# Forget gates of a hybrid attention layer: an addition and a running sum on VectorE become one scan with two additions

## The reference, cut to what matters

```python
log_f = jax.nn.log_sigmoid((f_logit + b_forget[layer]).astype(jnp.float32))
log_f_cum = jnp.cumsum(log_f.transpose(0, 2, 1), axis=-1)
...
logits = logits + log_f_cum[:, :, start:end, None] - log_f_cum[:, :, None, :end]
```

## Time and profile before

| | before |
|---|---|
| median of 3 runs | 803.08 us |
| the profiled execution | 803.57 us |
| its span, first to last instruction | 801.8 us |
| PE busy | 792.6 us (99%) |
| DVE busy | 580.4 us (72%) |
| ACT busy | 454.9 us (57%) |
| POOL busy | 239.2 us (30%) |
| share of PE in the chain that ended last | 94% |

### The profile page before, as it was taken

How to read it: one execution, slowest core, us unless ns; L and a number is a source line. 1 busy time by engine, 2 the same in 40 slices (tenths; PEclk the granted TensorE clock), 3 DMA queues, 4 the chain that set the end, 5 groups by cost and what they waited for, 6 DMA issues and landing times.

```text
span 801.8 us, 12113 instructions
## 1 busy us (share of the span) xinstructions
PE 792.6 (99%) x4184; PEld 671.3 (84%) x4184; DVE 580.4 (72%) x1178; ACT 454.9 (57%) x928; POOL 239.2 (30%) x378
## 2 busy tenths in 40 slices
PE   9999999999999999999999999999999999999997
PEld 8878888888888888888888888888888888888885
DVE  6877666676668887767788776779657677875575
ACT  7767665556647555665745576565546483542232
POOL 0112631342245225234533341454233111410000
PEclk9999999999999999999999999999999999999999
DMA  9414823114122411411061131104312298152532
GB/s 345 155 53 151 273 80 117 54 41 131 40 79 51 134 40 67 132 39 54 30 175 46 67 103 69 53 27 114 110 54 67 82 371 300 54 179 79 184 132 105
DMA packets 35276, 88.93 MB, mean 111 GB/s; under 512 B 3592, under 2 KB 11784, under 8 KB 34192
## 3 DMA queue, kind: packets, MB, share of 16 engines
q1 hardware_dynamic: 35216, 88.17, 33.3%
HBM read 57.72 MB, written 21.53 MB: 99 GB/s over the span
## 4 chain that ended last, share of the span: by engine, by line
PE 94%; DVE 2%; DMA 2%; issue 1%; ACT 1%; SPq 0%; ACTq 0%; DVEq 0%
PE banks L818 16%; PE banks L820 16%; PE banks L819 16%; PE banks L863 11%; PE banks L993 9%; PE banks L1013 5%; PE banks L980 5%; PE banks L1012 5%; PE banks L979 5%; PE banks L1064 1%; PE banks L950 1%; PE banks L945 1%; PE banks L1033 1%; DMA hT<-wo_dram 1%; PE banks L935 1%
## 5 line engine op out<-in xcount | busy, mean ns | idle before, releaser
L818 PE MATMUL banks<-hT,w_parts 128*128 128x512 f32 x576 | 237.3, 412 | 0.2 <-DVE sb_heads L1661 0.2
L820 PE MATMUL banks<-hT,w_parts 128*128 128x512 f32 x576 | 225.9, 392 | 0.0
L819 PE MATMUL banks<-hT,w_parts 128*128 128x512 f32 x576 | 225.4, 391 | 0.0
L1775 DVE TENSOR_TENSOR pT<-banks,pT 128x512 fp32r<-128x512 f32 x208 | 108.3, 563 | 88.9 <-ACT pT L1222 87.3
L1222 ACT ACTIVATE pT<-banks 128x512 fp32r<-128x512 f32 x208 | 92.5, 497 | 135.3 <-PE banks L993 135.1
L820 PEld LDWEIGHTS banks<-hT,w_parts 128*128 128x128 f32 x576 | 108.1, 188 | 24.5
L818 PEld LDWEIGHTS banks<-hT,w_parts 128*128 128x128 f32 x576 | 108.5, 188 | 15.0 <-DVE sb_heads L1661 0.7
L819 PEld LDWEIGHTS banks<-hT,w_parts 128*128 128x128 f32 x576 | 108.9, 189 | 13.3
L1490 POOL TENSOR_TENSOR w_parts<-w_raw,w_parts 128x1024 fp32r<-128x1024 f32 x34 | 81.5, 2398 | 95.9 <-ACT w_parts L1122 95.9
L1735 DVE TENSOR_TENSOR_SCAN work<-work 128x639 f32<-128x639 f32 (+3 forms) x64 | 90.6, 1416 | 4.7 <-POOL work L1497 4.6
L1198 ACT ACTIVATE work<-banks 128x512 f32<-128x512 f32 (+2 forms) x96 | 47.5, 495 | 71.0 <-PE banks L980 60.8
(11 more groups left out here) (248 smaller groups left out, 1366.3 us busy)
## 6 DMA issues: line engine op xcount, KB each, us to landing
w_raw<-in_w_tiles SPq DMA_DIRECT2D x36, 512.0 KB, 4.1
hT<-wo_dram SPq DMA_DIRECT2D x14, 512.0 KB, 8.0
fx_heads<-fx_heads SPq DMA_DIRECT2D x8, 512.0 KB, 7.5
negL<-negL_dram SPq DMA_DIRECT2D x8, 512.0 KB, 6.5
yT_dram<-silu SPq DMA_DIRECT2D x8, 512.0 KB, 5.1
sb_heads<-sb_heads SPq DMA_DIRECT2D x8, 512.0 KB, 7.0
negL<-yT_dram SPq DMA_DIRECT2D x8, 512.0 KB, 5.0
work<-in_x SPq DMA_DIRECT2D x6, 512.0 KB, 7.0
```

What stands on the lines that cost most here:

```text
L818: pe.matmul(o, w[0][:, k, :], hT[:, 0, k, tok], start=(k == 0), stop=False)
L819: pe.matmul(o, w[0][:, k, :], hT[:, 1, k, tok], start=False, stop=False)
L820: mm = pe.matmul(o, w[1][:, k, :], hT[:, 0, k, tok], start=False, stop=(k == KT - 1))
L1775: dve.tensor_tensor(pT[:, n % 3, 1, cols], banks[:, T_BANK + n % 2, cols], pT[:, n % 3, 0, cols].bitcast(F32), ALU.subtract).then_inc(t_lo, 1)
```

## The change

`f_one` and its filling (L1947) go. `forget_sum` goes, and `forget_scan` runs in tick 2 in place of tick 3, right behind ACT's logarithm: state = (f_a + state) + f_m. SP's store stands at its tick 3 in place of 4; its order of DMAs is the same as before.

```diff
-FORGET_SUM, FORGET_SCAN, FORGET_STORE = 2, 3, 4
+FORGET_SCAN, FORGET_STORE = 2, 3
...
-            def forget_sum():
+            def forget_scan():
+
                 dve.wait_ge(f_ln, 1)
-                dve.tensor_tensor(f_m, f_m, f_a, ALU.add).then_inc(f_sum, 1)
-
-            def forget_scan():
-                dve.wait_ge(f_sum, 1)
-                dve.tensor_tensor_scan(f_m, f_one, f_m, 0.0, ALU.mult, ALU.add).then_inc(f_scan, 1)
+                dve.tensor_tensor_scan(f_m, f_a, f_m, 0.0, ALU.add, ALU.add).then_inc(f_scan, 1)
...
-            link(dve.memset(f_one, 1.0))
             forget_begin(0)
...
-                if i == FORGET_SUM:
-                    forget_sum()
                 if i == FORGET_SCAN:
                     forget_scan()
```

More of the change, by code:

```diff
@@ L450, in hybrid_layer @@
         junk, junk_dve = pT[:, 0, :, :], pT[:, 1, :, :]
-        f_u, f_one, f_a, f_m = work[0:FH, S:2 * S], work[0:FH, 2 * S:3 * S], f_row(0)[0:FH, :], f_row(1)[0:FH, :]
+        f_u, f_a, f_m = work[0:FH, S:2 * S], f_row(0)[0:FH, :], f_row(1)[0:FH, :]
         wo_rows = [(silu[:, :], negL[:, 0, :])] + [(raw, fx_heads[:, i * S:(i + 1) * S].bitcast(F32)) for raw, i in
@@ L512, in hybrid_layer @@
         wf_hi, wf_lo = sem("wf_hi"), sem("wf_lo")
-        f_abs, f_exp, f_ln, f_sum, f_scan, negL_out = sem("f_abs"), sem("f_exp"), sem("f_ln"), sem("f_sum"), sem("f_scan"), sem("negL_out")
+        f_abs, f_exp, f_ln, f_scan, negL_out = sem("f_abs"), sem("f_exp"), sem("f_ln"), sem("f_scan"), sem("negL_out")
         negL_in = [sem("negL_in0"), sem("negL_in1")]
```

## The result

The changed kernel takes 804.59 us (median of 22 runs, 803.6 to 805.36), the kernel before 803.34 us (median of 22, 802.88 to 804.12): a ratio of 1.0013, with a 95% interval of 1.0007 to 1.0019. (The medians differ by 1.25 us, a quotient of 1.0016; the ratio is not taken from them alone, and its interval holds both.) It is slower by 0.6 to 1.5 us, which is less than the 0.2% that the text ahead calls no change; still, with 22 runs of each, a ratio of 1 lies outside the interval. The profiled execution took 804.53 us with a span of 802.8, where the one before had 803.57 and 801.8.

A forecast was written before the change was run, and what follows sets the result against it. PE, busy 792.6 of 801.8 us, was taken as the bound, with DVE counting only where PE waits. Terms -0.35 + 1.3 + 0 = +0.95 us on the 803.08 median gave 804.03, predicted 804.0, range 802.5 to 804.8.

The forecast's parts named there:

- The two waits of PE: PE's waits for DVE at L818 (0.35 us late) and L1012 (0.48 us late), together at most 0.83 us to gain.
- The maximum of unit 3: DVE's result that ACT's exponential awaits; predicted 1.00 us later, since what stands between units 2 and 3's maxima sets time.
- The scan takes 2.27 us, held it ends 2.14 behind POOL: DVE's new scan at about 65.3 us, 2.27 us by itself, held by POOL's subtraction L1490, ending at 69.04.
- The stall at unit 5: New PE wait of some 1.3 us at the scores of unit 5, for ACT's exponential of unit 3.
- The terms of the sum: On PE: -0.35 at L818, +1.3 at the scores of unit 5 (the 0.35 included), 0 at L1012: +0.95 us.
- The filling gives its 0.35 back: Removing DVE's 0.91 us filling ahead of L1661 gains 0.35 us at L818, given back at the scores of unit 5.
- the logarithm's chain: Steps behind the last forget logits, up to 65 us; predicted at most 0.14 us earlier without the filling, 0.05 taken.
- The scan that is not held: Rival: POOL does not hold the scan, it ends at 67.61, maximum of unit 3 0.43 us earlier; 802.65 us, chance 0.12.
- the slow scan: Rival: two additions make the scan slower, up to 3.34 us, for +2.02 or 805.10 us; chance 0.08.
- Both waits of PE gone: Rival: keys do not hang on ACT's queue, so all 0.83 us at L818 and L1012 is gained; 802.25 us, chance 0.04.
- SP's store is worth nothing: SP's store goes at about 69.1 in place of 70.77; read only from tick 32, so no gain.
- The fetch that moves along with PE: PE's only wait after 74 us, 0.7 us, for a fetch SP issues when PE reaches a point of its program.

## Why the prediction was right

It forecast 804.0 us in 802.5 to 804.8, a loss of 0.95 us; measured were 804.59 and a loss of 1.25 (0.6 to 1.5).

- **The two waits of PE are all that can be gained.** The mechanism is shown: with the scan in tick 3 both are gone. But the 0.83 us that the text calls the most that PE can gain was too small: PE gained 0.94 us at L1012 and 1.09 behind it. It left out that the matmuls behind a wait also come late, by 0.1 us and more (55.37 behind 55.03 is 0.34 us, and 54.80 behind 54.58 is 0.22 with the wait gone).
- **The maximum of unit 3 sets the time.** Shown from three sides: more work between the scan and it costs in full, the scan behind it costs nothing, and its earlier end (POOL moved away) comes through to L1012.
- **The scan takes 2.27 us, held it ends 2.14 behind POOL.** Forecast 69.04, found 68.86 + 0.09 = 68.95. The 0.09 between them are in the start of POOL's subtraction: 64.32 + 0.09 is 0.15 us earlier than before, where I had taken 0.05 out of at most 0.14. That made the maximum of unit 3 0.1 us less late than forecast, and with it most of the difference between 0.95 and 0.89 at L1012.
- **The stall at unit 5.** Forecast 1.3 us, found 1.22.
- **The terms of the sum.** Forecast -0.35 + 1.3 + 0 = +0.95. Against the same matmuls before, PE stood 0.50 us earlier behind L818 (for 0.35), lost 1.22 at the scores of unit 5 and 0.1 with the matmul behind (1.3, as forecast), and 0.09 at L1012 (for 0): +0.89, some hundredths being rounding. What PE gains more at L818 it only loses again in the stall, and L1012 waits in both kernels, so that its place follows that of L1669, 0.89 us later (72.02 + 0.09 for 71.22). That is why the sum came out closer than its terms.
- **The filling gives its 0.35 back.** Right in the main. With the filling kept, POOL's subtraction and the scan behind it end 0.17 us later and L1012 0.18 us later, so that the logarithm's chain keeps 0.18 of what is removed.
- **Rivals.** The scan that is not held, and the slow scan, are both ruled out by runs. Both waits of PE gone was held to need L1669 free of ACT; in fact moving the scan alone does it, since ACT's queue then moves up by 2.7 us against the changed kernel as well.
- **SP's store is worth nothing.** Right for an earlier store. What the text did not look at is the other direction: 5.6 us later, it costs PE 4.9 us, not by the store but by the loads behind it: a stall of 3.15 us with 0.1 us behind it, and 1.7 us in matmuls at half the clock.
- **The fetch that moves along with PE.** Not borne out in single executions: the wait at L863 was 0.69 us before and 0.78 after, and in the other ten traces anything from none to 0.87, in no order by how early PE was.

The forecast of 804.03 us lies 0.56 under the 804.59 measured. Of this, 0.26 us are not in the change: the median before was 803.08 in the 3 runs that the forecast started from, and 803.34 in 22. The other 0.30 is the loss, 1.25 for 0.95. The 0.36 us between the loss at L1012 (0.89) and that of the medians (1.25) lies inside the interval, and stays open: the two profiled executions differ by 0.96 us, and in them PE's lag stays between 0.80 and 0.89 to 400 us and is 1.09 at the end.

## What to carry to other kernels

Where one engine is busy for 99% of the span, the worth of a change on another engine is read from the waits between the two: which result is late, and which instructions stand ahead of it in its engine's order. Merging two instructions can be a loss when the longer single one lands ahead of a result that is waited for, and moving it behind that result, at no cost in work, moved PE up by 1.83 us here (24.89 to 23.06). A duration stretched by another engine's hold does not go with the instruction: here the scan that took the addition's place inherited the hold, while a filling at that place did not.

## What the runs showed of the hardware that was not expected

- A float32 scan on DVE takes the same with two additions, with product and sum, and with one addition alone: 2.27 us for 8 partitions by 1024 elements in three kernels, near the 2.28 of 128 partitions by 1023.
- A filling on DVE (8 x 1024, 0.91 us) is not held by POOL's subtraction, although the scan right behind it is.
- After a wait of 2.98 us PE's granted clock fell to 0.50 (the level of 1.2 GHz) for 3.3 us, from 1.3 us behind the end of the wait on, and that cost 1.7 us more (addition in tick 3, scan in tick 6). After waits of 1.06 us (changed kernel) and 2.15 us (filling behind the scan) it stayed at 1.00. Nothing else was varied here, so what brings it down is not shown.
- The hold goes both ways. Where a scan of DVE began 0.09 us ahead of POOL's subtraction of output weights (scan in tick 4), POOL took 4.37 us for what takes 2.38 in the changed kernel, and ended 2.19 us behind the scan. With the addition in tick 3 and the scan in tick 4 it took 4.39 us likewise. DVE's timeline of that kernel:

```profile
68.43 2.27 DVE L1839 TENSOR_TENSOR_SCAN work<-work 8x1024 f32<-8x1024 f32 x1
```

and POOL's:

```profile
68.52 4.37 POOL L1526 TENSOR_TENSOR silu<-silu,negL 128x1024 fp32r<-128x1024 f32 x1 [1.53 <-ACT negL L1304]
```
